# Picking expert rows from x itself, and new orders at the routing and at the end of a mixture-of-experts block

## The reference, cut to what matters

```python
h = rms_norm(x, norm_ffn)
group = argmax(softmax(h @ w_rg + b_rg))              # 4 groups
top_p, top_i = top_k(softmax((h @ w_re + b_re)[group]), 2)   # of 8 experts in the group
weights = p_group_top * top_p / sum(top_p)
y = sum over the token's two experts e of weights[e] * ((silu(h @ w_g[e]) * (h @ w_u[e])) @ w_d[e])
out = x + y
```

## Time and profile before

| | |
|---|---|
| median of three runs | 701.91 us |
| the profiled execution's own time | 701.26 us |
| its span | 699.1 us |
| TensorE matmul busy | 615.8 us, 88% |
| VectorE, ScalarE, GpSimd busy | 279.8, 199.6, 28.5 us |
| read from HBM | 245.72 MB, 353 GB/s over the span |
| the chain that ended last | PE 57%, DMA 40% |
| granted TensorE clock, mean | 0.948 |

### The profile page before, as it was taken

The page is one execution under the profiler, slowest core; times in us unless marked ns, Lnnn a source line. Parts: engine busy times, 40 slices in busy tenths (PEclk is TensorE's granted clock), DMA queues, the critical chain, the costliest instruction groups (busy, mean ns, idle before and its releaser), DMA issues.

```text
span 699.1 us, 11551 instructions
## 1 busy us (share of the span) xinstructions
PE 615.8 (88%) x4690; PEld 373.8 (53%) x4690; DVE 279.8 (40%) x623; ACT 199.6 (29%) x334; POOL 28.5 (4%) x54
## 2 busy tenths in 40 slices
PE   8999999999999998999987788775878857797876
PEld 5887899999999893333332233322323323332333
DVE  6476976985474945333231112211112211120311
ACT  5684455473535433121111111111111111110111
POOL 2612000000000020000000000000000000000000
PEclk9999999999999999999997989999889998887999
DMA  9995347436479799999999999999999999999995
GB/s 314 309 373 185 133 139 221 155 133 229 166 272 420 304 387 398 428 424 426 429 426 427 429 427 427 427 425 427 428 427 429 425 428 427 428 425 429 426 419 211
DMA packets 40388, 247.53 MB, mean 354 GB/s; under 512 B 4456, under 2 KB 6640, under 8 KB 26128
## 3 DMA queue, kind: packets, MB, share of 16 engines
q1 hardware_dynamic: 37872, 245.44, 86.6%
q0 software_dynamic: 912, 1.25, 1.0%
q10 hardware_dynamic: 1552, 0.10, 0.2%
HBM read 245.72 MB, written 1.06 MB: 353 GB/s over the span
## 4 chain that ended last, share of the span: by engine, by line
PE 57%; DMA 40%; DVE 1%; issue 1%; SPq 0%; POOL 0%; POOLq 0%; DVEq 0%
DMA wide<-in_w_expert_up 35%; PE ps L1431 9%; PE ps L1048 6%; PE ps L1049 6%; PE ps L1050 6%; DMA wide<-in_w_expert_down 5%; PE ps L1468 3%; PE ps L1023 3%; PE ps L1025 3%; PE ps L1024 3%; PE ps L1442 2%; PE ps L1524 2%; PE ps L1079 2%; PE ps L1395 1%; PE ps L1404 1%; PE ps L1091 1%
## 5 line engine op out<-in xcount | busy, mean ns | idle before, releaser
L1431 PE MATMUL ps<-wide,xe 128*32 128x512 f32 x1024 | 147.5, 700 | 72.0 <-DMA wide<-in_w_expert_up 70.2
L2083 DVE TENSOR_TENSOR he<-g_s,ps 128x128 f32<-128x128 f32 x32 | 9.2, 289 | 267.1 <-ACT g_s L935 264.2
L1431 PEld LDWEIGHTS ps<-wide,xe 128*32 128x32 f32 x1024 | 31.2, 119 | 145.0 <-issue 128.8
L1603 DVE TENSOR_TENSOR ring_lo<-ring,w_hi 128x1024 fp32r<-128x1024 f32 x76 | 91.3, 1222 | 41.4 <-ACT w_hi L742 41.0
L742 ACT ACTIVATE w_hi<-ring 128x1024 fp32r<-128x1024 f32 x76 | 78.9, 1057 | 54.8 <-PE ps L1050 34.9
L935 ACT ACTIVATE g_s<-ps 128x128 f32<-128x128 f32 x32 | 8.9, 277 | 252.1 <-PE ps L1442 252.1
L1048 PE MATMUL ps<-hT_hi,w_hi 128*128 128x256 f32 x288 | 80.4, 279 | 0.0
L1049 PE MATMUL ps<-hT_lo,w_hi 128*128 128x256 f32 x288 | 79.5, 276 | 0.0
L1050 PE MATMUL ps<-hT_hi,ring_lo 128*128 128x256 f32 x288 | 79.5, 276 | 0.0
L1524 PE MATMUL ps<-y,back 64*128 64x512 f32 x240 | 59.6, 611 | 1.9 <-ACT y L943 0.9
L1468 PE MATMUL ps<-wide,he 128*32 128x512 f32 x472 | 56.8, 598 | 0.0
(11 more groups left out here) (288 smaller groups left out, 790.9 us busy)
## 6 DMA issues: line engine op xcount, KB each, us to landing
wide<-in_w_expert_gate SPq DMA_DIRECT2D x27, 2048.0 KB, 46.8
wide<-in_w_expert_up SPq DMA_DIRECT2D x27, 2048.0 KB, 48.9
wide<-in_w_expert_down SPq DMA_DIRECT2D x26, 2048.0 KB, 42.5
ring<-in_w_in SPq DMA_DIRECT2D x8, 2048.0 KB, 14.7
ring<-in_w_merge_gate SPq DMA_DIRECT2D x6, 2048.0 KB, 8.7
wide<-in_w_expert_gate SPq DMA_DIRECT2D x10, 1024.0 KB, 9.4
wide<-in_w_expert_up SPq DMA_DIRECT2D x10, 1024.0 KB, 13.5
wide<-in_w_expert_down SPq DMA_DIRECT2D x10, 1024.0 KB, 10.1
```

Source lines behind the costliest of these rows:

```text
L1431: ins = t_.matmul(ps[q * WIN:(q + 1) * WIN, b, :], xe[b][:, j % 2, 2 * c + j // 2, :], w[:, C * j:C * (j + 1)], start=(c == 0 and j < 2), ...
L1603: v.tensor_tensor(piece(ring_lo, g, c), piece(ring, g, c), by_row(out_hi[g == 19][c]).bitcast(F32), ALU.subtract).then_inc(wpre_lo, 1)
```

## The change

The two copies and their semaphores are gone. `pick_rows` reads `x_tok` itself, with a step of 8 elements, and the inverse root is multiplied into `pick_w`: for the first expert on the column `stat[:, 44:46]`, for the others in `one_row`, ahead of which a new instruction `join` adds the two choices. `scr`, `w_al`, `zT` and `reset` now lie where `x_tok` was, `x_tok` has room of its own for good, and unit 20 goes where `scr` and its neighbours are. It waits for a nop behind the first square sums and moves in the order from the last place to behind 16. The final copies go into `x_tok`.

On TensorE `out_quarter_low` is split from `out_quarter`, and the turns and router products of the last pieces stand in another order; on ScalarE the copies of the turned pieces follow it. On VectorE `in_group(0)` and `best_two(0)` move ahead of `x1_add(1, 2)`, and `eh` behind the first `pick_w`. The register loads of the number of passes move from expert 1 to expert 8 (`COUNT_AT`) on TensorE, ScalarE and VectorE.

At the end the last unit comes in two rows of k, [128 x 1024] each; `down_last(p, i)` takes row i for all four quarters; one copy and one `combine_last` in two rounds over all four quarters follow. ScalarE's own queue stores tokens 128 to 255, SyncE's the others.

```diff
 RING = 22
 EXTRA = 22
+COUNT_AT = 8
 UNITS = 6 * NE
 LAST = (slice(0, 2 * QW), slice(2 * QW, D))
-LAST_Q = ((0, 1), (2, 3))
...
         w_hi_at = top[0]
         w_hi = [place(f"w_hi{c}", [P, CW], F32R) for c in range(CHUNKS)]
-        x_at = top[0]
+        top[0] += 192
+        scr_at = top[0]
+        scr = place("scr", [P, 2, C], F32)
+        w_al_at = top[0]
+        w_al = place("w_al", [P, 256], F32)
+        zT = place("zT", [P, T], F32)
+        top[0] += 1024
+        reset = place("reset", [P, T], F32)
+        xn_at = top[0]
+        assert xn_at - scr_at == 4 * UNIT
+        xn = place("xn_merged", [P, TT, D], F32)
         x_tok = place("x_tok", [P, TT, D], F32)
-        xn_at = top[0]
-        xn = place("xn_merged", [P, TT, D], F32)
         merged_lo = place("merged_lo", [P, KD, T], F32R, at=xn_at)
         ident = place("ident", [P, P], F32)
...
-        w_al_at = top[0]
-        w_al = place("w_al", [P, 256], F32)
-        zT = place("zT", [P, T], F32)
-        top[0] += 1024
-        reset = place("reset", [P, T], F32)
-        assert top[0] - w_al_at == 4 * D
         table = place("table", [BUCKETS, NH], F32)
...
-        scr_at = here_at[0]
-        scr = here("scr", [P, 2, C], F32)
+        late_at = here_at[0]
...
-        xn2_at = (scr_at, w_al_at)
-        xn2 = [place(f"xn2_{tt}", [P, D], F32, at=at) for tt, at in enumerate(xn2_at)]
-        fin = [place(f"fin{tt}", [P, D], F32, at=at) for tt, at in enumerate(xn2_at)]
-        junk = [xn2[0], place("junk", [P, C], F32, at=w_al_at)]
+        fin = [x_tok[:, tt, :] for tt in range(TT)]
+        squares = [place("squares_half", [P, C], F32, at=scr_at)]
+        squares += [place("squares_quarter", [P, QW], F32, at=late_at)] * 2
...
-        unit_at += [ring_at[4], ring_at[4] + 4 * UNIT, gv_at, gv_at + 4 * UNIT, x_at, xn_at]
+        unit_at += [ring_at[4], ring_at[4] + 4 * UNIT, gv_at, gv_at + 4 * UNIT, scr_at, xn_at]
...
                 if m == len(moves) - 1:
-                    for i, cols_i in enumerate(LAST):
-                        sp.dma_start(unit[j].rearrange("p (k n) -> p k n", n=D)[:, :, cols_i],
-                                     src[e, :, c * UNIT:(c + 1) * UNIT].rearrange("p (k n) -> p k n", n=D)[:, :, cols_i]
+                    for i in range(2):
+                        sp.dma_start(unit[j][:, D * i:D * (i + 1)], src[e, :, c * UNIT + D * i:c * UNIT + D * (i + 1)]
...
-                elif n != 20:
+                elif n == 20:
+                    sp.wait_ge(halves_squared, 1)
+                else:
                     sp.wait_ge(proj_done, first_bank[NPRE - 2] + 6)
-                else:
-                    sp.wait_ge(seeded, 1)
-                    sp.wait_ge(xn0_ready, 1)
-                    sp.wait_ge(xn1_ready, 1)
...
-            for n in [0, 1, 2, 3, 11] + list(range(4, 11)) + [12, 14, 13, 15, 16, 18, 17, 19, 21, EXTRA, 20]:
+            for n in [0, 1, 2, 3, 11] + list(range(4, 11)) + [12, 14, 13, 15, 16, 20, 18, 17, 19, 21, EXTRA]:
...
             for i, cols_i in enumerate(LAST):
-                for tt in range(TT):
-                    sp.wait_ge(fin_act if tt else fin_dve, i + 1)
-                    sp.dma_start(out[0, tt * P:(tt + 1) * P, cols_i], fin[tt][:, cols_i]).then_inc(stored, 16)
+                sp.wait_ge(fin_dve, i + 1)
+                sp.dma_start(out[0, 0:P, cols_i], fin[0][:, cols_i]).then_inc(stored, 16)
...
-            pool.wait_ge(rstd_ready, 1)
-            g.tensor_scalar(xn2[0][:, :].rearrange("p (k f) -> p k f", k=KD), x_tok[:, 0, :].rearrange("p (f k) -> p k f", k=KD),
-                            stat[:, 40:41], None, ALU.mult).then_inc(xn0_ready, 1)
...
-            x1T_out(1, 4, 6, 4)
-            x1T_out(0, 6, 8, 5)
+            x1T_out(0, 6, 8, 4)
+            x1T_out(1, 4, 6, 5)
             x1T_out(1, 6, 8, 6)
             x1_root(1)
-            act.wait_ge(proj_done, first_bank[NPRE - 2] + 6)
-            act.wait_ge(rstd_ready, 2)
-            s_.activation(xn2[1][:, :].rearrange("p (k f) -> p k f", k=KD), x_tok[:, 1, :].rearrange("p (f k) -> p k f", k=KD),
-                          ACT.Copy, scale=stat[:, 41:42]).then_inc(xn1_ready, 1)
...
-                for i, qs in enumerate(LAST_Q):
-                    if i == 0:
-                        act.wait_ge(last_done, p + 1)
-                    else:
-                        act.wait_ge(unit_free, after(p, "d", NE - 1))
-                    rows_i = slice(WIN * qs[0], WIN * (qs[-1] + 1))
-                    s_.activation(y_end[rows_i, :], ps[rows_i, 0, 0:QW], ACT.Copy,
-                                  scale=w_slot[rows_i, (NE - 1) % 2:(NE - 1) % 2 + 1]).then_inc(y_last_ready, 1)
+                act.wait_ge(unit_free, after(p, "d", NE - 1))
+                s_.activation(y_end[:, :], ps[:, 0, 0:QW], ACT.Copy,
+                              scale=w_slot[:, (NE - 1) % 2:(NE - 1) % 2 + 1]).then_inc(y_last_ready, 1)
...
-                act.wait_ge(route_ready, 1)
-                act.reg_load(passes, npass[0:1, 0:1])
-                turns = act.value_load(npass[0:1, 0:1], min_val=1, max_val=MAXWIN)
                 for e in range(1, NE - 1):
+                    if e == COUNT_AT:
+                        act.wait_ge(route_ready, 1)
+                        act.reg_load(passes, npass[0:1, 0:1])
+                        turns = act.value_load(npass[0:1, 0:1], min_val=1, max_val=MAXWIN)
...
+            for i, cols_i in enumerate(LAST):
+                act.wait_ge(fin_act, i + 1)
+                act.dma_start(out[0, P:T, cols_i], fin[1][:, cols_i]).then_inc(stored, 16)
...
+            def out_quarter_low(tt, q):
+
+                out_begin(tt, q)
+                for k in range(KD):
+                    ins = t_.matmul(bank(2 * q + tt)[:, 0:QW], merged_hi[:, k, tt * P:(tt + 1) * P], low_row(q, k),
+                                    start=(k == 0), stop=False)
+                ins.then_inc(chunk_done, 1)
+
...
+            out_quarter_low(1, 0)
...
-            out_quarter(1, 1, range(0, 2))
+            out_quarter_low(1, 1)
+            turn_x1(0, range(6, KD), 5)
             turn_x1(1, range(4, 6), 4)
-            turn_x1(0, range(6, KD), 5)
-            out_quarter(1, 1, range(2, 5))
-            route(0, range(6, KD), 5)
-            out_quarter(1, 1, range(5, KD))
-            route(1, range(4, 6), 4)
+            out_quarter(1, 1, range(0, 3))
+            route(0, range(6, KD), 4)
+            out_quarter(1, 1, range(3, KD))
+            route(1, range(4, 6), 5)
...
-                        ins = t_.matmul(ps[q * WIN:(q + 1) * WIN, e % 2, 0:QW], pick_w[e % 2][:, tt, :], xn2[tt][:, QW * q:QW * (q + 1)],
+                        rows_q = x_tok[:, tt, :].rearrange("p (f k) -> p k f", k=KD)[:, 2 * q:2 * q + 2, :]
+                        ins = t_.matmul(bank(e % 2, 4)[q * WIN:(q + 1) * WIN, 0:2, :], pick_w[e % 2][:, tt, :], rows_q,
...
-            pe.wait_ge(xn0_ready, 1)
-            pe.wait_ge(xn1_ready, 1)
...
-                for j in range(2):
-                    for q in LAST_Q[i]:
-                        ins = t_.matmul(ps[q * WIN:(q + 1) * WIN, 0, 0:QW], he[:, 2 + j, :],
-                                        u[:, D * j + QW * q:D * j + QW * (q + 1)], start=False, stop=(j == 1))
-                if i == 0:
-                    ins.then_inc(last_done, 1)
-                else:
+                for q in range(NQ):
+                    ins = t_.matmul(ps[q * WIN:(q + 1) * WIN, 0, 0:QW], he[:, 2 + i, :],
+                                    u[:, D * i + QW * q:D * i + QW * (q + 1)], start=False, stop=(i == 1))
+                if i == 1:
...
-            def combine_last(p, i):
+            def combine_last(p):
 
                 pe.wait_ge(back_ready, NE * p + (NE + 1))
-                pe.wait_ge(y_last_ready, 2 * p + (i + 1))
-                combine_quarters(p, NE - 1, LAST_Q[i], y_end)
+                pe.wait_ge(y_last_ready, p + 1)
+                combine_quarters(p, NE - 1, range(NQ), y_end)
 
...
+            v.engine_nop().then_inc(halves_squared, 1)
...
+            in_group(0)
+            best_two(0)
             x1_add(1, 2)
             square_sum(1, 2)
             mean_square(1)
-            in_group(0)
             scale_out(1)
-            best_two(0)
             group_of(1)
             in_group(1)
...
+            link(v.tensor_tensor(stat[:, 44:46], stat[:, 44:46], stat[:, 40:42], ALU.mult))
             every = iota_f[:, :].unsqueeze(1).unsqueeze(1).broadcast_to([P, TT, TOPK, NE])
             chosen = ie8[:, :, 0:TOPK].unsqueeze(3).broadcast_to([P, TT, TOPK, NE])
-            v.tensor_tensor(eh[:, :, :, :], every, chosen, ALU.is_equal).then_inc(assign_ready, 1)
             dve.wait_ge(pos_mm, 1)
             for tt in range(TT):
                 ins = v.scalar_tensor_tensor(out=pick_w[0][:, tt, :], in0=iota_w[:, :], scalar=ps[:, 2, tt:tt + 1],
                                              in1=stat[:, 44 + tt:45 + tt].broadcast_to([P, WIN]), op0=ALU.is_equal, op1=ALU.mult)
```

(42 more changed lines are left out.)

30 lines of the change are left out of this document (11 added, 19 removed).

## The result

Six executions of the changed kernel took 705.08 us in the median (704.05 to 705.86), six of the kernel before 701.60 (700.95 to 702.41): a ratio of 1.0048, 95% interval 1.0036 to 1.0060. The profiled execution took 704.64 us, its span is 702.6 us. So the change made the kernel 3.5 us slower, outside the predicted range.

What follows compares the result with a forecast made beforehand. From 280 us weights arrive at a fixed 427 GB/s, so only the stream's start and the end count. Stream +0.2 and end 0 on 701.26 profiled, with 0.65 to the median, gave 702.1, rounded 702.0; range 700.3 to 703.3.

Steps and rivals of the forecast that it cites:

- decided between 225 and 275 us: Start of the weight stream: how early its queue is full was said to be settled in this window; nothing counted ahead.
- The strided pick: First pick, on the path to load 22: reading x with a step of 8 fp32 was put at +0.4 us.
- rival 2: Strided pick is dear: 2.2 us (+1.1, end 702.8) or +3.2 (704.9); chance of over 0.2% slower 0.15.
- later picks cost the end nothing: Picks after the first lie where the stream is ahead, so their strided reads were put at no cost.
- The routing's order: Routing ahead of the first pick: TensorE 0.5 us earlier, VectorE's addition 0.4 late, the first pick 0.3 late.
- Load 22: First load of the stream's steady part, gate of expert 4; forecast to land 0.2 us later than before.
- unexplained 1.3 us: Part of load 22's landing time before the change that no row explained; the forecast assumed it stays.
- rival 1: Load 22's slow start vanishes too, giving 700.2 us; chance 0.2 together with the reordering gaining up to its cap of 1.3.
- Terms two and three: Distances from down units 8 and 9's issue to load 22's, and on to its landing; forecast for the stream: 0.2 us later.
- End: Behind the last landing: last unit in two rows of k, final copies, stores on two queues; forecast 0 in sum.
- The pass count: Reading it at expert 8 instead of 1: forecast cost 0, or 1.2 us without cover by loads already out.
- The stated marks: Signs of right or wrong in the later profile: unit 20's and load 22's issue, load 22's landing, the pick's duration.

Runs made afterwards that it cites:

- h3: Changed kernel with one transpose of ident into an idle PSUM bank ahead of the first branch product; 701.84 us, ratio 1.0004.
- g2: Changed kernel with four transposes of ident into an idle PSUM bank ahead of the first branch product; 702.01 us, ratio 1.0001.
- g1: Changed kernel with four transposes of ident into an idle PSUM bank behind the first branch product; 702.74 us, ratio 1.0016.
- e3: Kernel before, with yc_hi, an operand of the branch product, moved from byte 223808 to 132512; 702.49 us, ratio 1.0009.
- f3: Kernel before, with scr, and with it yc_hi, placed 256 bytes higher; 701.92 us, ratio 1.0000.
- e6: Changed kernel with VectorE's routing steps back in the order of before; 704.03 us, ratio 1.0037.

## Why the prediction was wrong

- **Upstream (not in the sum at all).** The step that failed is the first of the prediction, that the start of the stream "is decided between 225 and 275 us": what lies ahead was put at nothing, because the change adds no instruction there. It costs +2.47 us in the profiled executions, more than all other terms together, and with the 0.5 us by which this one came earlier and the 0.2 behind the stretch about 3.2. With the quick rhythm the changed kernel takes 701.84 (h3) or 702.01 us (g2), and 702.0 was the forecast; that it comes out so near is in part luck, as the next points show. What in the change brings the slower rhythm on is open. It is no chance of the single execution: the changed kernel and all eight made from it without transposes have it from 155 us on, and g1 up to its transposes; of before only e3 is slow there, and leaves it at 166 us. GpSimd's early end, yc_hi's place alone and a shift by 256 bytes are out. The weights of these products lie where they lay before, the tiles streamed against them lie 4352 bytes higher; that shift, and the other numbers of the semaphores, were not tried alone. The shift is not needed for such a rhythm: f3 has a slow stretch, at 102 us, without it.
- **The strided pick.** Right in kind, +0.4 taken, +0.96 measured. I went by the nearest row, the weight load; ScalarE's factor of two in the earlier trace rows was the right one: 2.03/1.07 = 1.9, and 636/379 ns over all picks, close to rival 2's first price of 2.2 us. By the Trainium skill, SBUF — State Buffer (Door 1: The DMA port swizzle), fp32 steps by 4 are free and longer ones pay. The trace agrees that a step of 8 pays, 2.03 us against 1.07; no run has a step of 4. The forecast that later picks cost the end nothing holds as far as the traces tell: 412.90 us of stream in both, and 412.6 to 413.8 over all traces.
- **The routing's order.** Right, in kind and size. The 0.3 was the net of TensorE's 0.5 won and VectorE's later addition. In g2, in the quick rhythm, group_of(0) starts 0.6 us earlier behind the down units than before the change, the addition 0.37 later (0.4 predicted) and pick_w 0.28 later. e6's 0.38 is VectorE's order alone: of the two moves it is the one that loses, since the addition that the other token half waits for now stands behind half 0's last steps.
- **Load 22.** I let its unexplained 1.3 us stay. It went: 9.59 to 8.08 us behind the issue, where 7.8 and the 1.3 would have made 9.1. That is rival 1's mechanism as far as the time goes, with the gap at 255 filled as predicted. Terms two and three give -0.12 us on balance, where I had +0.2: nearly right, by two errors that cancel.
- **End.** 0 predicted, +0.3 measured, all of it from the rows of k (I had +0.15 for the chain and -0.1 for the packets). The 2.25 us from the last of these matmuls to the first final copy are as added up; it is the matmuls that end 0.68 us behind the last landing in e6 (694.46), where I had about 0.5. The second queue was given 0.15 and brings 0. I put ScalarE's issues behind both its copies; its queue issued the first store from 697.99, while the copies ran.
- **The pass count**: 0, as predicted, as far as the table can tell. TensorE's idle time ahead of expert 1's first gate_up was 1.68 us and is 1.02 now, waiting for VectorE's `fold`.
- **The stated marks.** "Load 22 issued after 270.5" said wrong (272.68), but only through the upstream loss: in the quick rhythm it is 270.28 (g2), between the marks for right and for wrong. The pick of 2.03 missed the 1.4 to 1.5 for right and stayed just under the 2.1 for wrong, and the landing of 8.08 just over its 8. The mark that caught the loss is unit 20's issue, set near 247.8: it came at 250.32, 2.5 us late.

## What to carry over

Where a kernel is changed in one place, compare the pace of the untouched stretches first, count by window and duration by line: here they held more than two thirds of the loss. A long unbroken run of matmuls can be in a slower rhythm, depending on how it is entered; one cheap matmul of another shape ahead of it is worth a trial. Reading a tile with a long step in place of making a packed copy moves the cost from engines that had time for it to the one on the path.

## What the runs showed of the hardware

- Alternating 128x128 weight loads and 256-column fp32r matmuls at full granted clock have two steady spacings, 113.4 and 117.8 ns (records of 276 and 281 ns). The slower one held for 79 us, and ended at a break of the stream where one was made (g1); what chooses between them is open.
- A pick of 16 matmul records with a moving step of 32 bytes takes 2.03 us, packed 1.07.
- A stretch of half clock (granted 0.50) that ends 14 to 25 us ahead of the end costs 0.7 to 1.7 us at the end, even in a part that waits for DMA: expert 31's up product took 3.56 us in the changed kernel's trace for 1.92 in e6's, and TensorE did not catch up. It may be part of the spread of a microsecond and a half between executions of one kernel; only profiled ones show where their half-clock stretches lie.
